# The modulation vector of a two-stack transformer kernel as one stream of 72 chunks over five FFNs

## What is computed

```python
def modulate(x, shift, scale):
    return x * (1 + scale[:, None, :]) + shift[:, None, :]

for l in range(DEPTH):                       # DEPTH = 2
    mod = (jax.nn.silu(c) @ ada_w[l] + ada_b[l]).reshape(b_, N_SUB, 3, D_MODEL)   # 9 x 1024 numbers
    y = swiglu(modulate(x, mod[:, 0, 0], mod[:, 0, 1]), ffn_w13[l, 0], ffn_w2[l, 0])
    x = layer_norm(ALPHA * x + 0.5 * (1 + mod[:, 0, 2])[:, None, :] * y, ...)
    y = token_mixer(modulate(x, mod[:, 1, 0], mod[:, 1, 1]), ...)
    x = layer_norm(ALPHA * x + (1 + mod[:, 1, 2])[:, None, :] * y, ...)
    y = swiglu(modulate(x, mod[:, 2, 0], mod[:, 2, 1]), ffn_w13[l, 1], ffn_w2[l, 1])
    x = layer_norm(ALPHA * x + 0.5 * (1 + mod[:, 2, 2])[:, None, :] * y, ...)
```

## Time and profile before

| | us |
|---|---|
| median of 3 runs | 2133.96 (2132.45 to 2134.3) |
| span of the profiled execution | 2129.5 |
| PE busy | 1950.1 (92%) |
| DVE busy | 1385.7 (65%) |
| ACT busy | 964.7 (45%) |
| POOL busy | 153.1 (7%) |
| `w_lo` on DVE, L1568, x270 | 617.0, mean 2290 ns |
| `w_hi` on ACT, L1154, x270 | 508.9, mean 1887 ns |
| bytes read from HBM | 370.45 MB, 174 GB/s over the span |

### The profile page before, as it was taken

How to read it: one execution, slowest core, us unless ns; L and a number is a source line. 1 busy time by engine, 2 the same in 40 slices (tenths; PEclk the granted TensorE clock), 3 DMA queues, 4 the chain that set the end, 5 groups by cost and what they waited for, 6 DMA issues and landing times.

```text
span 2129.5 us, 33332 instructions
## 1 busy us (share of the span) xinstructions
PE 1950.1 (92%) x12850; PEld 1774.1 (83%) x12850; DVE 1385.7 (65%) x2147; ACT 964.7 (45%) x1479; POOL 153.1 (7%) x202
## 2 busy tenths in 40 slices
PE   7988999898899989998997999996999898899997
PEld 6867899677789978997877889985999787888996
DVE  4486778538678777667646575547766754757545
ACT  5454544455544444344544344343433645334332
POOL 0000000000000000002003320000000200512000
PEclk9999999999999999999999899997999999989999
DMA  7115786411487748863420145545876351024552
GB/s 280 46 56 209 295 309 242 158 64 60 168 316 274 278 181 333 299 231 123 153 99 1 42 173 195 183 158 233 304 268 219 109 171 57 1 83 177 193 182 77
DMA packets 54069, 372.91 MB, mean 175 GB/s; under 512 B 5968, under 2 KB 6864, under 8 KB 10832
## 3 DMA queue, kind: packets, MB, share of 16 engines
q1 hardware_dynamic: 51392, 361.45, 46.2%
q0 software_dynamic: 2016, 9.07, 1.2%
q10 hardware_dynamic: 560, 0.99, 0.1%
HBM read 370.45 MB, written 1.05 MB: 174 GB/s over the span
## 4 chain that ended last, share of the span: by engine, by line
PE 77%; DVE 11%; ACT 4%; DMA 4%; issue 3%; SPq 0%; DVEq 0%; POOLq 0%; ACTq 0%
PE bank L628 12%; PE bank L630 12%; PE bank L629 12%; PE bank L708 5%; PE bank L709 5%; PE bank L710 5%; PE bank L667 4%; PE bank L668 4%; PE bank L669 4%; DVE w_lo L1568 2%; DMA raw<-in_wa 2%; PE bank L1080 2%; DMA raw<-in_wb 2%; PE bank L1089 2%; PE bank L1088 1%
## 5 line engine op out<-in xcount | busy, mean ns | idle before, releaser
L628 PE MATMUL bank<-hT_hi,w_hi 128*128 128x256 f32 x2432 | 696.8, 287 | 13.5 <-DVE w_lo L1568 13.1
L1568 DVE TENSOR_TENSOR w_lo<-raw,w_hi 128x2048 fp32r<-128x2048 f32 (+2 forms) x270 | 617.0, 2290 | 120.6 <-ACT w_hi L1154 120.1
L629 PE MATMUL bank<-hT_lo,w_hi 128*128 128x256 f32 x2432 | 692.8, 285 | 0.0
L630 PE MATMUL bank<-hT_hi,w_lo 128*128 128x256 f32 x2432 | 692.4, 285 | 0.0
L1154 ACT ACTIVATE w_hi<-raw 128x2048 fp32r<-128x2048 f32 (+2 forms) x270 | 508.9, 1887 | 268.8 <-PE bank L710 101.2
L628 PEld LDWEIGHTS bank<-hT_hi,w_hi 128*128 128x128 f32 x2432 | 469.9, 193 | 20.9 <-DVE w_lo L1568 16.4
L629 PEld LDWEIGHTS bank<-hT_lo,w_hi 128*128 128x128 f32 x2432 | 469.8, 193 | 3.3 <-issue 0.5
L630 PEld LDWEIGHTS bank<-hT_hi,w_lo 128*128 128x128 f32 x2432 | 469.5, 193 | 0.5
L708 PE MATMUL bank<-w_hi,hid_hi 128*128 128x512 f32 x528 | 210.8, 399 | 22.1 <-DVE w_lo L1568 15.7
L709 PE MATMUL bank<-w_lo,hid_hi 128*128 128x512 f32 x528 | 209.0, 396 | 0.0
L710 PE MATMUL bank<-w_hi,hid_lo 128*128 128x512 f32 x528 | 208.3, 395 | 0.0
(11 more groups left out here) (360 smaller groups left out, 2443.7 us busy)
## 6 DMA issues: line engine op xcount, KB each, us to landing
raw<-in_wb SPq DMA_DIRECT2D x168, 1024.0 KB, 5.0
raw<-in_wa SPq DMA_DIRECT2D x96, 1024.0 KB, 4.9
scratch<-in_wm SPq DMA_DIRECT2D x72, 1024.0 KB, 6.7
lnw<-in_ln_g POOLq DMA_DIRECT2D x6, 512.0 KB, 4.1
lnw<-in_ln_b POOLq DMA_DIRECT2D x6, 512.0 KB, 5.9
cst<-in_const POOLq DMA_DIRECT2D x1, 2205.0 KB, 9.7
raw<-in_wa SPq DMA_DIRECT2D x4, 512.0 KB, 3.6
scratch<-in_c SPq DMA_DIRECT2D x4, 512.0 KB, 4.5
```

Source lines behind the costliest of these rows:

```text
L628: nc.tensor.matmul(out, ah, bh, start=(i == 0), stop=False)
L629: nc.tensor.matmul(out, ah, bl, start=False, stop=False)
L630: last = nc.tensor.matmul(out, al, bh, start=False, stop=(i == n - 1))
L1568: nc.vector.tensor_tensor(w_lo[:, slot, 0:width], raw[:, raw_slot, 0:width], w_hi[:, slot, 0:width].bitcast(F32), ALU.subtract).then_inc(l ...
```

## The change

- `SUB`, `ADA_ALL`, `ADA_F`: the 72 chunks become one stream. FFN number f of F1 to F5 takes chunks 15 f to 15 f + 14, F5 (f = 4) the last 12. F4, which had none, now has 15.
- SP loads positions 0 to 3 and then `c`, then position 4, and behind every second weight position from 4 on (4, 6, ... 32) one modulation chunk. The SP loops are unrolled. The wait for the free region stands behind position 3 in place of position 2; F4 waits for `B["nx"]`.
- DVE computes no column between `post(0)` and the turns. Turn j computes the columns of chunk group j in the places where group j+1 stood; F5 has a loop of four turns with columns and one turn without.
- ACT makes silu(c) five times in place of four (F4 too).
- `moda` holds all 144 columns. The bias of the first sublayer is kept in `ada_b0` and added when a layer of `B` starts, in place of a copy from `mod`. The constant `pair` (384 of the constants' columns) goes; `pair12` serves for it.

The core of the diff:

```diff
-ADA_N = MOD2 // 2
-ADA_T = ADA_N // RING
+SUB = 3 * KT
+ADA_ALL = DEPTH * MOD // 2
+ADA_F = (FFN_N // RING // 2) * RING
@@ SP
+            def load_ada(g):
+                if g >= RING:
+                    sp.wait_ge(ada_used, g - RING + 1)
+                sp.dma_start(ada_raw[:, g % RING, :], t["wm"][g // (MOD // 2), g % (MOD // 2), :, :]).then_inc(ada_in[g % RING], 16)
+            def load_ffn(f, load, free=None):
+                for pos in range(RING + 1):
+                    load(pos)
+                if f is not None:
+                    free()
+                    sp.dma_start(cb, t["c"].partition_broadcast(P)).then_inc(c_in, 16)
+                for pos in range(RING + 1, FFN_N):
+                    load(pos)
+                    g, late = divmod(pos - RING - 1, 2)
+                    if f is not None and not late and g < ADA_F and f * ADA_F + g < ADA_ALL:
+                        load_ada(f * ADA_F + g)
@@ SP, second block
-                with sp.Fori(0, FFN_N // RING) as j:
-                    for r in range(RING):
-                        load_b(sp, l, j, B_S0["ffn1"], r)
+                load_ffn(DEPTH + 1 if l == 0 else None, lambda pos: load_b(sp, l, B_S0["ffn1"] + pos),
+                         lambda: sp.wait_ge(B["nx"], 2 * TT))
@@ DVE, turn
-                        if part is not None:
+                        if columns:
                             for k in ((), (0,), (1, 2), (), (3,), (4, 5))[q]:
-                                ada(j + 1, k)
+                                ada(j, k)
@@ DVE, ffn
-                early = 1 if conv else 0
-                if early:
-                    dve.wait_ge(c_silu, part + 1)
-                    ada(0, 0)
                 post(0, 0, 0, lambda: None)
-                if part is not None:
-                    dve.wait_ge(c_silu, part + 1)
-                    for k in range(early, 2 * RING):
-                        ada(0, k)
-                with dve.Fori(0, (FT - 2) // 4) as j:
-                    turn(j)
+                turns = (FT - 2) // 4
+                full = 0 if f_mod is None else min(turns, (ADA_ALL - f_mod * ADA_F) // RING)
+                if full:
+                    dve.wait_ge(c_silu, f_mod + 1)
+                    with dve.Fori(0, full) as j:
+                        turn(j, True)
+                if full < turns:
+                    with dve.Fori(full, turns) as j:
+                        turn(j, False)
@@ DVE, start of a layer of B
-                link(nc.vector.tensor_copy(modl[:, 0:MOD2], mod[:, bass.ds(l, 1), :].rearrange("p o n -> p (o n)")))
+                dve.wait_ge(ada_used, (DEPTH + 2 * l) * ADA_F)
+                link(nc.vector.tensor_tensor(modl[:, 0:SUB], moda[:, l * MOD:l * MOD + SUB], ada_b0[:, l, :], ALU.add))
```

More of the change, by code:

```diff
@@ L143, in _constants @@
     put("quad_of", (i // 32 == np.arange(4)[None, :]).astype(np.float32))
[L144 to L147, removed]
     pair12 = np.zeros((12, 6, P), np.float32)
@@ L239, in build @@
         spa = sb("spa", [P, max(DEPTH * SA_W, SB_W)])
-        moda = sb("moda", [P, MOD2])
-        mod = sb("mod", [P, DEPTH, MOD2])
+        moda = sb("moda", [P, DEPTH * MOD])
+        ada_b0 = sb("ada_b0", [P, DEPTH, SUB])
         modl = sb("modl", [P, MOD])
@@ L1587, in lo_features, with ffn @@
                                                    op0=ALU.mult, op1=ALU.subtract).then_inc(N["tp_lo"], 1)
-            def ffn(N, split, h0, more, conv=False, part=None):
+            def ffn(N, split, h0, more, conv=False, f_mod=None):
                 def post(f, f2, f4, ahead):
@@ L1610, in ada, with turn @@
                     if half == 0:
-                        dve.wait_ge(ada_in[r], part * (16 * ADA_T) + j * 16 + 16)
-                    last = modulation(ada_raw[:, r, :], half, moda[:, bass.ds(j * (2 * RING) + k, 1)])
+                        dve.wait_ge(ada_in[r], j * 16 + (f_mod * (16 * ADA_F // RING) + 16))
+                    last = modulation(ada_raw[:, r, :], half, moda[:, bass.ds(j * (2 * RING) + (f_mod * 2 * ADA_F + k), 1)])
                     if half:
                         last.then_inc(ada_used, 1)
-                def turn(j):
+                def turn(j, columns):
                     for q in range(6):
@@ L1907, in _ @@
                 lo_features(A, 2, "g2")
-                ffn(A, split + (A_WIN + A_WOUT), 0, 0, conv=True, part=l)
-                dve.wait_ge(ada_used, l * ADA_N + ADA_N)
-                nc.vector.tensor_tensor(mod[:, bass.ds(l, 1), :].rearrange("p o n -> p (o n)"), moda[:, :], sa("ada_b"), ALU.add)
+                ffn(A, split + (A_WIN + A_WOUT), 0, 0, conv=True, f_mod=l)
+                nc.vector.tensor_copy(ada_b0[:, l, :], sa("ada_b"))
                 for i in range(TT):
@@ L2050, in _ @@
                 gate_diagonal(0)
-                ffn(B, split, 0, 0, part=l + DEPTH)
+                ffn(B, split, 0, 0, f_mod=DEPTH + 2 * l)
                 dve.wait_ge(small_in, l * 16 + 32)
-                dve.wait_ge(ada_used, (l + DEPTH) * ADA_N + ADA_N)
-                link(nc.vector.tensor_tensor(modl[:, MOD2:MOD], moda[:, :], sbp("ada_b"), ALU.add))
+                dve.wait_ge(ada_used, min((DEPTH + 2 * l + 1) * ADA_F, ADA_ALL))
+                link(nc.vector.tensor_tensor(modl[:, SUB:MOD], moda[:, l * MOD + SUB:(l + 1) * MOD], sbp("ada_b"), ALU.add))
                 link(nc.vector.tensor_scalar(by_kind[:, 1:3, 1:3, :], by_kind[:, 1:3, 1:3, :], 1.0, None, ALU.add))
```

44 lines of the change are left out of this document (18 added, 26 removed).

## The result

The changed kernel takes 2104.11 us (median of 4 runs, 2101.35 to 2113.01) against 2133.2 (4 runs, 2129.26 to 2134.3); the ratio is 0.9874, 95% interval 0.985 to 0.9898. Measured twice more beside the kernel before, it was 0.9871 (0.9841 to 0.99) and 0.9881 (0.9859 to 0.9902). One execution of the changed kernel, of 16, took 4453.81 us, which nothing here explains; the ratios leave it out. The change gains 1.2 to 1.3%, some 25 to 29 us.

A forecast was written before the change was run, and what follows sets the result against it. PE was taken to bound the kernel, losing time in four FFN heads: 3.35 + 5.35 + 3.95 + 9.55 = 22.2 us, all other terms 0. 2133.96 - 22.2 = 2111.8 us, range 2106.5 to 2120.

The forecast's parts named there:

- PE bounds the kernel, and the loop has nothing to give: Whole kernel: PE has 77% of the chain; in mid-F1 34.00 us of a turn hold 34.00 us of PE.
- The heads are where the time goes: Heads of F1, F2, F3, F5: PE waits 2.2, 3.0, 2.3 and 7.5 us for `w_lo`; all four waits costed at zero afterwards.
- The prediction's cross-check: Four heads: 15.0 us of waits leave 7.2 of the 22.2 us, 1.8 per FFN, for the slow clock behind them.
- The reference: FFN length without columns: 182.55 us from F4 and F6, 184.25 with gate matmuls in F3 and F5; excess 22.2 us.
- Both parts of the delay count: Heads: a weight chunk behind three modulation loads, then a `lo` behind six columns, as two delays in a row.
- The turns would pay nothing: Turns: cost 0, gain 0; 10.5 us remain for a modulation chunk against landings of 4.8 to 7.4 us.
- one of the prediction's own signs of being wrong: Turns: a wait of DVE's L1562 for `in_wm` would show the forecast wrong.
- The rival: Turns: column 2 waits for a late chunk ahead of `lo`; 3.6 us in 24 turns, 86 us, 2198; chance 0.04.
- F4 costs nothing: F4 newly gets `c`, silu(c) and 30 columns: cost 0, slack 2.6 us in its first turn, at worst 6 us.
- some 1.5 us later: F4's first turn: column 2 at 358 GB/s instead of 426 would be this much later, leaving 1.1 us slack.
- Everything outside the FFNs at nothing: Outside the FFNs: small parts 0 to 0.2 us gained; clock at the ends of F1 and F2 1.5 us either way each.
- 4.46 us lie around the span: Whole kernel: the median lies 4.46 us above the profiled span, so span 2107.3 became the forecast 2111.8.

The follow-up runs named there:

- late-load kernel: Each modulation load issued two weight positions later, against the changed kernel; 2230.67 us, ratio 1.047 to the kernel before.
- loads-back kernel: SP's old load order restored in the heads of F1, F2, F3 and F5 of the changed kernel, columns left in the turns; 2112.25 us, repeated 2108.48.
- POOL held back: POOL's two elementwise steps on x delayed in the changed kernel until hid_lo of tile 2: in F4 and F6 2107.7 us, in F6 alone 2109.61.
- columns twice: A second multiply-and-sum of the same size beside each column of the changed kernel; 2136.62 us, ratio 1.0009 to the kernel before.
- columns back: First six columns put back behind post(0) in F1, F2, F3 and F5 of the changed kernel, position 3's early load kept; 2131.19 us, ratio 0.999.

## Why the forecast gain was too small, point by point

- **PE bounds the kernel, and the loop has nothing to give: right.** A steady turn is 34.00 us of PE before and after, and the kernel without modulation has the same FFN lengths within 0.4 us in sum.
- **The heads are where the time goes: right. A slow clock behind each wait but F1's: right in one profile of before; in the repeated one behind F5's alone.** 24.5 of 29.7 us of the spans' difference are the FFNs, and no wait for `w_lo` is left in the heads of F1, F2, F3 and F5 in any of the three profiles. The prediction's cross-check put 1.5 to 3 us of slow clock on each head as if it always followed. Here are 3 us behind F2's wait, of 3.0 us in the first profile and of 2.8 in the repeated one:

```profile
595.10:598.10 3.00, 2.92 (x8) 1.71 (x6) 0.85 (x2) 2.50 (x4) 0.00 (x0) 0.50 1.00 423
```
```profile
596.40:599.40 3.00, 2.39 (x11) 1.61 (x9) 0.85 (x2) 2.49 (x4) 0.00 (x0) 1.00 1.02 431
```

- **The reference was mis-sized, the first failing step: 22.2 us forecast, 24.5 measured in the FFNs, 23.8 with the changed kernel's last profile and 22.8 with a repeated profile on both sides.** I took F4 and F6 as free of stalls because they have no columns. They are not. PE waits 0.85 us for a `w_lo` in F4 of before, whose POOL and `w_lo` stand in the earlier trace rows; F6 of before has no such wait, but starts with 2.7 us at the lower clock. The changed kernel's F6 waits 0.7 us for a `w_lo` that took 6.72 us, and holding POOL back took 1.0 us off it. F1 and F2 came out at 181.3 and 181.8, and in the repeats at 182.1 and 181.2 or 181.3, not at 182.55. Some 1.4 of the 24.5 us is chance on top: 2.9 us less of the lower clock at the starts of F1 and F2 in the changed kernel's first profile. I used the row for F4's cost and not for the reference.
- **Both parts of the delay count: half right, and weighted wrongly.** The prediction put the late weight chunk first and the six columns second. The columns in their old place bring back 18.7 us of FFN length (some of it by the loads' order in that kernel), the old load order alone 1.3 to 2.1 us, and the old load order on top of the old columns about 5.8. In F1 ACT had idled only 0.5 us for position 3; I showed the argument on F5, where ACT's wait is longest, and let it stand for four.
- **The turns would pay nothing: right.** DVE waits once for a modulation chunk in the whole execution, 1.0 us (1.1 and 1.6 in the repeats), in F4's first turn at column 2. That was one of the prediction's own signs of being wrong, but PE does not wait behind it, and the working had it: a chunk that lands at 1277.2 against a column that could start at 1275.7, 1.5 us. The rival did not occur. Its price, 3.6 us per turn at a landing of 15.4 us, was not tested; the late-load kernel shows that such a delay costs more than PE's direct wait.
- **F4 costs nothing: right** (182.9 against 182.8; 182.5 and 182.9 in the repeats). The rule of the Trainium skill's page "DMA: Bandwidth & Descriptors", section Specifications, about 358 GB/s per core from HBM, was weighed there; stretches of 3 us moved 369 and 401 GB/s in this profile, so the measurement decides against it as a ceiling here, and it made no difference. The prediction's "some 1.5 us later" by that figure does not come out: 1 MB at 358 GB/s is an estimate of 2.9 us against 2.5, which is 0.5 us later and leaves a slack of about 2 us.
- **Everything outside the FFNs at nothing: the second failing step, and the larger one.** The span was forecast at 2107.3 us and is 2099.8: 2.3 of these 7.5 us are the reference, 5.2 lie outside the FFNs, where I allowed 1.5 us of clock at the end of each of F1 and F2 and nothing elsewhere. Runs of one program spread by more than 10 us, and the stretch ahead of F1 alone by 3.7. Each pairing of a profile of before with one of the changed kernel has such a rest, 3.4 to 5.7 us, but not in the same stretches. Nor is it tied to the change: outside the FFNs the two profiles of before have 1008.6 and 1008.3 us, the changed kernel's three 1002.8 to 1004.9, and the loads-back kernel's two 1011.9 and 1005.6, though its edit lies in the FFNs' heads alone. Whether any of it belongs to the change stays open. The ratios of the three measurements are 0.987 to 0.988. The forecast as a ratio, 2111.8 / 2133.96 = 0.9896, lies inside all three intervals, near their upper ends. The medians of the repeats, 2106.81 and 2105.75, lie at the lower end of the range or just below it, so it was in part chance that the first median, of four runs, lay 2.4 us outside.
- **"4.46 us lie around the span": wrong.** Measured on executions with both numbers, it is 1.8 us after (2101.59 and 2099.8) and 2.1 before (2130.38 and 2128.3). The profiled execution of before was itself, by this estimate, 2 to 3 us faster than its median. It did no harm by luck: the changed kernel's median also stands 4.3 us above its profiled span.

What stays open: what sets the granted clock outside the FFNs in a given execution. The profiles show that it differs and by how much, not why.

## What to carry to other kernels

Side work in an in-order queue costs nothing in a steady loop with slack; in a head it costs what goes beyond the slack there, and the clock that may fall behind the wait. So put its first piece one turn later rather than ahead of the first product. When two delays end in one wait, remove each alone on the chip before crediting either: here one was worth most of the gain and the other 1 to 2 us alone, and some 6 with the first in place. A reference stretch must be read for its own waits before a difference is taken against it, and a forecast in us needs the spread of repeated runs in its range, not only the unknown terms.

## What the runs showed of the hardware that I had not expected

- Two profiles of one unedited program put the same first stretch at 189.3 and 193.0 us. Over 15 executions of it the mean granted clock lies between 0.955 and 0.965 and the span between 2111.2 and 2096.1 us.
- A `w_lo` that starts while POOL's elementwise step runs mostly ends 2.1 us after that step does: 6.77 us in place of 2.28 in the earlier trace rows, 6.70 when the step is moved into F4's first turn, 4.37 where less of the step was left (F6, POOL held back). It can go the other way: in F4 of before two `w_lo` in a row, the first of them begun 0.2 us ahead of the step, took their usual 2.28 us each, and the step took 8.8 us in place of 6.6. Moving the step moves the delay.
- Waits of up to 1.0 us per down chunk in every turn (columns twice) left the granted clock at its upper level. Single waits of 1.9 to 3.0 us did either: the lower clock followed those of 2.3 and 3.0 us in F3 and F2 of before and of 2.6 us in F5 (columns back), and did not follow those of 2.2 us in F1 of before, 2.8 us in F2 of its repeated profile and 1.9 us in F3 (columns back).
